# Small constant buffers placed ahead of the matmul operands h_hi and h_lo

## What is computed

```
def swiglu(h, w_gate_up, w_down):          # h: 256 x 1024, inner width 2816
    gate, up = jnp.split(h @ w_gate_up, 2, axis=-1)
    return (jax.nn.silu(gate) * up) @ w_down
```

## Time and profile before

| | |
|---|---|
| median of 3 runs | 2812.49 us (2812.39 to 2812.81) |
| the profiled execution, its own time | 2811.96 us |
| span from its first to its last instruction | 2810.1 us |
| mean granted clock of TensorE | 0.971 |
| busy: TensorE, VectorE, ScalarE, GpSimd | 94%, 66%, 45%, 10% |
| read from HBM | 426.80 MB, 153 GB/s over the span |

### The profile page before, as it was taken

The page is one execution under the profiler, slowest core; times in us unless marked ns, Lnnn a source line. Parts: engine busy times, 40 slices in busy tenths (PEclk is TensorE's granted clock), DMA queues, the critical chain, the costliest instruction groups (busy, mean ns, idle before and its releaser), DMA issues.

```text
span 2810.1 us, 51613 instructions
## 1 busy us (share of the span) xinstructions
PE 2653.0 (94%) x21578; PEld 2571.6 (92%) x21578; DVE 1841.9 (66%) x2279; ACT 1267.4 (45%) x1489; POOL 285.1 (10%) x419
## 2 busy tenths in 40 slices
PE   7998854999999999999999999999999999999998
PEld 6998744999999988998999999999999999999998
DVE  3756777655666675554656656986656656996655
ACT  3434322533456565333434334665434334665433
POOL 7000481000300010000000000140000000230000
PEclk9999877999999999999999999999999999999999
DMA  4454101454567773553554544443554554443543
GB/s 167 179 179 165 31 1 30 151 189 184 157 171 159 159 167 106 180 183 113 180 189 167 195 179 159 153 146 143 181 179 168 191 181 157 154 146 142 182 179 120
DMA packets 77780, 433.01 MB, mean 154 GB/s; under 512 B 20224, under 2 KB 22784, under 8 KB 27728
## 3 DMA queue, kind: packets, MB, share of 16 engines
q1 hardware_dynamic: 58720, 410.25, 40.0%
q0 software_dynamic: 5888, 17.53, 5.1%
q10 hardware_dynamic: 13040, 3.34, 0.6%
HBM read 426.80 MB, written 3.24 MB: 153 GB/s over the span
## 4 chain that ended last, share of the span: by engine, by line
PE 86%; DVE 8%; ACT 2%; POOL 2%; issue 1%; DMA 1%; ACTq 0%; DVEq 0%; POOLq 0%
PE psum L1854 25%; PE psum L1856 25%; PE psum L1855 25%; PE psum L2143 1%; PE psum L1953 1%; PE psum L1887 1%; DVE w_lo L1309 1%; PE psum L2119 1%; PE psum L2131 1%; ACT w_hi L850 1%; DVE arena L1479 1%; DVE arena L1484 1%; PE psum L2122 1%; PE psum L1939 1%; DVE rstd L1334 0%
## 5 line engine op out<-in xcount | busy, mean ns | idle before, releaser
L1854 PE MATMUL psum<-h_hi,w_hi 128*128 128x256 f32 x4320 | 1236.6, 286 | 32.5 <-DVE h_lo L1347 15.1
L1856 PE MATMUL psum<-h_hi,w_lo 128*128 128x256 f32 x4320 | 1226.6, 284 | 0.0
L1855 PE MATMUL psum<-h_lo,w_hi 128*128 128x256 f32 x4320 | 1226.5, 284 | 0.0
L850 ACT ACTIVATE w_hi<-raw 128x2048 fp32r<-128x2048 f32 x387 | 740.2, 1913 | 930.4 <-PE psum L1856 930.4
L1309 DVE TENSOR_TENSOR w_lo<-raw,w_hi 128x2048 fp32r<-128x2048 f32 x387 | 891.2, 2303 | 393.9 <-ACT w_hi L850 393.9
L1854 PEld LDWEIGHTS psum<-h_hi,w_hi 128*128 128x128 f32 x4320 | 832.7, 193 | 44.0 <-issue 34.5
L1855 PEld LDWEIGHTS psum<-h_lo,w_hi 128*128 128x128 f32 x4320 | 832.7, 193 | 1.2 <-issue 1.0
L1856 PEld LDWEIGHTS psum<-h_hi,w_lo 128*128 128x128 f32 x4320 | 832.4, 193 | 0.0
L1854 PE MATMUL psum<-act_hi,w_hi 128*128 128x256 f32 x1536 | 431.4, 281 | 1.9 <-DVE w_lo L1309 1.2
L1855 PE MATMUL psum<-act_lo,w_hi 128*128 128x256 f32 x1536 | 428.6, 279 | 0.0
L1856 PE MATMUL psum<-act_hi,w_lo 128*128 128x256 f32 x1536 | 428.6, 279 | 0.0
(11 more groups left out here) (311 smaller groups left out, 2704.7 us busy)
## 6 DMA issues: line engine op xcount, KB each, us to landing
raw<-in_panels SPq DMA_DIRECT2D x387, 1024.0 KB, 4.8
arena<-bias_by_distance POOLq DMA_DIRECT2D x32, 384.0 KB, 7.8
x<-in_x SPq DMA_DIRECT2D x1, 1024.0 KB, 7.4
arena<-in_dft_sq ACTq DMA_DIRECT2D x2, 512.0 KB, 6.1
arena<-in_s_b SPq DMA_DIRECT2D x1, 1024.0 KB, 15.2
arena<-in_s_c SPq DMA_DIRECT2D x1, 1024.0 KB, 16.8
arena<-s_u POOLq DMA_DIRECT2D x1, 1024.0 KB, 5.2
arena<-arena POOLq DMA_DIRECT2D x32, 32.0 KB, 1.9
```

Source lines behind the costliest of these rows:

```text
L850: a.activation(w_hi[:, s, :], raw[:, s, :], ACT.Copy).then_inc(hi_ready, 1)
L1854: t.matmul(o, w[0], xin[0], start=start, stop=False, skip_group_check=True)
L1855: t.matmul(o, w[0], xin[1], start=False, stop=False, skip_group_check=True)
L1856: return t.matmul(o, w[1], xin[0], start=False, stop=stop, skip_group_check=True)
```

## The change

Six calls of `sb` are moved ahead of those of `h_hi`, `h_lo` and `rstd`. The same buffers with the same sizes are allocated; nothing that an engine executes is altered but the addresses.

```
         x = sb("x", [P, KT, S])
         h = sb("h", [P, KT, S])
-        h_hi = sb("h_hi", [P, KT, S], F32R)
-        h_lo = sb("h_lo", [P, KT, S], F32R)
-        rstd = sb("rstd", [P, S])
         gains = sb("gains", [P, A["gains"].shape[1]])
         ones = sb("ones", [P, P])
         zeros = sb("zeros", [P, P], F32R)
         eps = sb("eps", [P, 1])
         eps_head = sb("eps_head", [P, 1])
         warm = sb("warm", [P, 1])
+        h_hi = sb("h_hi", [P, KT, S], F32R)
+        h_lo = sb("h_lo", [P, KT, S], F32R)
+        rstd = sb("rstd", [P, S])
 
         hidden = sb("hidden", [P, 2, 2, 2, S])
```

## The result

The changed kernel takes 2773.65 us (median of 4 runs: 2778.99, 2777.73, 2769.57, 2769.33) against 2812.44 us before (4 runs). The ratio is 0.9863, with a 95% interval from 0.9846 to 0.9879. The profiled execution took 2778.99 us and has a span of 2777.2 us, 32.9 us less than before. The forecast was 2783.5 us with a range from 2779 to 2814.

A forecast was written before the change was run, and what follows sets the result against it. TensorE, busy 94% of the span, was taken as the bound through mm3's matmul spacing. Gains of 30.6 us less 1.6 eaten in the mix stages gave 29.0: 2812.49 - 29.0 = 2783.5 us, range 2779 to 2814.

The forecast's parts named there:

- The expected signs: FFN loop panels: 96 h starts in 11.31 us, weight loads under h at 188 ns, each FFN some 2.3 us shorter.
- no change: Rival for mm3: act is faster for lying above byte 131,072, which h stays below; 2812.5 us, chance 0.24.
- a slower kernel: Rival for mm3: h's start half-way between multiples of 128 bytes lengthens each of 13,920 matmuls; 2843 us, chance 0.06.
- Below 117.8 there would have to be something that act's own panels don't have: For matmuls with h moving, act's 117.8 ns taken as the best pace: 2.2 ns each, 28.5 us.
- FFNs 18.6 us forecast: Eight FFN stages, TensorE busy throughout: 1,056 h matmuls each gain 2.2 ns, 18.6 us with nothing in the way.
- Mix stages 6.1 - 1.6 = 4.5: Two mix stages: 6.1 us from the faster pace, less 0.8 us each where VectorE is nearly full.
- The forecast wait: Mix stages: a faster TensorE arrives early at VectorE's results and waits, as at L2235; 0.8 us per stage.
- Dilated stage 4.2: Dilated stage: 4.2 us gained and kept, since VectorE is busy only 224.13 of 358.40 us.
- the 2.2 ns that I took for them: Matmuls with h as weights: the same 2.2 ns gain at offset -64, 960 of them, 2.1 us, between 0 and that.
- Fourier and S5, 1.6 together: S5 stage's panels and the two Fourier stages: 0.8 us each from the faster h pace.
- Outside the stages 0 forecast: Matmuls with ones and VectorE and ScalarE operations on moved buffers: both costed at nothing, within +-0.4 us.
- The rule: TensorE's independent read ports for moving operand and weights never wait, so distance has no effect: sum 0, 2812.5 us.

The follow-up runs named there:

- all five profiles of the changed kernel: The changed kernel's first profile and four more of it unaltered; the repetitions measured medians 2772.24 and 2783.27 us, single executions 2779.28 and 2783.62 us.
- 192-byte kernel: Against the kernel before, h and act both placed 192 bytes from the weights' multiple of 512; 2741.36 us (2 runs), run again 2724.00 us (5 runs).
- the one with everything at 0: Against the kernel before, h_hi and h_lo moved above byte 131,072 and act below, both at distance 0 from the weights; 2821.96 us, ratio 1.0036.
- 480-byte kernel: Against the kernel before, h and act both at distance 480 bytes, with gains ahead of h_hi; 2796.01 us (2 runs), ratio 0.9942.
- 32-byte one: Against the kernel before, h and act both at distance 32 bytes, with eps alone ahead of h_hi; 2777.02 us (4 runs), ratio 0.9861.

## Why the prediction was right and wrong

**The reading was right.** A matmul of `mm3` sets the time, its pace depends on the buffer of its operand, and 64 bytes between h and the weights' grid give h the pace of act: 120.0 to 117.8 ns, as forecast. The expected signs came, the weight loads at 189 ns (188 expected), 11.31 us for the loop's 96 starts and an FFN 2.2 to 2.3 us shorter (the two early ones 1.8). The rivals of no change and of a slower kernel fell with the result, and h above byte 131,072 shows that the side brings h nothing by itself.

**The step that failed** is "Below 117.8 there would have to be something that act's own panels don't have", and the range's lower end of 2780 (2779) us that hung on it. Act's panels in fact stood at the same distance, and at that distance there is a second steady pace, 113.3 ns. The pace of act was a value seen in one surrounding, and I used it as a floor. In the profiled execution the second pace took the S5 panels: 51.0 to 47.2 us, where 0.8 us were forecast. Of the 3.0 us more, 1.5 are the second pace and 1.6 the granted clock of the first panel, which is luck. With the single panels elsewhere, some 700 matmuls ran at 113.3 ns in this execution, about 3 us; in others it takes a whole FFN.

Why act never showed it is open. Before, act's panels in an FFN follow panels of h at distance 0 without a break, and in the kernels with one distance for both the pace changes only across a break; that act needed a break is the nearest reading. It isn't that act's runs were short. In the changed kernel single panels between two breaks run at 113.3 ns, as this one of the dilated stage (33 steps in 3.74 us).

```profile
761.05 0.28 PE L1854 MATMUL psum<-h_hi,w_hi 128*128 128x256 f32 x1
...
764.79 0.28 PE L1854 MATMUL psum<-h_hi,w_hi 128*128 128x256 f32 x1
```

In the profile of before, nine runs of 24 or 48 act matmuls do begin after a break of 1.5 us or more, and all nine run at 117.8 ns; eight of them, in the output panels of the mix stages, have 117.8 in all five profiles of the changed kernel too.

**The other terms, against the profiled execution.** FFNs 18.6 us forecast, 17.2 measured. Mix stages 6.1 - 1.6 = 4.5, measured 5.1. There the steady stretches gained 3.5 and 3.3 us, a part of it at 113.3 ns, and 1.7 us were lost again in the first stage and nothing in the second. The forecast wait didn't grow (L2235 for L1703: 2.9 us before, 2.6 after), so the total came out near for other reasons than the stated one. Dilated stage 4.2, measured 3.4, and here a part was mis-sized: the panels with h as weights, 576 of its 1,920 matmuls, gained nothing (120.0 ns as before), so the 2.2 ns that I took for them was wrong there, 1.3 us. For the 384 in the mix stages it was right. Fourier and S5, 1.6 together, measured 4.6. Outside the stages 0 forecast, 2.6 measured and not explained. The sum was 29.0, and the profiled execution lost 33.0 us (2811.96 to 2778.99), which is at the edge of the range. The median lies another 5 us lower through runs that no profile shows. The second pace is large enough for that, but the profiles with a fast FFN, 2778.72 and 2779.28 us, were no shorter than the first, so the cause of these 5 us stays open.

**The rule.** The 192-byte kernel and the one with everything at 0 differ by 81 to 98 us (2741.36 and 2724.00 against 2821.96) with the same instructions, so the trace disagrees with what the Trainium skill ("SBUF — State Buffer", Who interferes with whom) says of TensorE's two read ports, if that is read to mean that the operands' places can't matter. The runs show that the pace depends on the distance between the moving operand and the weights (120.0, 117.8 or 113.3 ns). They don't show that the two reads collide; this is the nearest reading, since neither address alone does it and exchanging the roles at the same addresses changes the pace.

## What to carry to other kernels

When the same matmul has two paces in one trace, compare operands that share a loop, then ask where their buffers lie to each other: here 192 bytes of padding are worth 3% of a kernel that is bound by TensorE. Try several distances on the chip, and with all operands at the same one, since the dependence has no simple form within its 256 bytes. The best pace seen in one surrounding is not a floor, and a pace that is drawn anew in each execution needs several runs and more than one profile.

## What was not expected of the hardware

- Back-to-back fp32r matmuls of 256 columns settle into steady paces: 120.0 ns at distances 0, 96 and 256; 118.3 at 48 and 480; 118.6 at 128; 117.4, 118.6 or 120.0 at 160; 116.7 or 117.8 at 32; 117.8 or 113.3 at 64 and 192.
- Where there are several, one is kept for as long as nothing interrupts the stream, up to a whole FFN of 1,584 matmuls. In ten profiles of kernels with one distance for h and act no unbroken stretch of 60 matmuls or more changes its pace. A wait of 1.5 us was enough to change it, and in the dilated stage a break of 0.57 us between two starts, in which other matmuls run. The granted clock reads 1.00 in both.
- The distance counts with its sign and modulo 256 bytes. With the roles exchanged, the contiguous weights of the mix stages give the pace of the opposite distance (116.7 ns in the 480-byte kernel, 118.3 in the 32-byte one); the dilated stage's panels, whose weights are read in steps of two elements, stayed at 120.0 ns at a distance of minus 64.
